# Two changes of order around the output blocks: a root of one number ahead of the statistics, and norm products inside the last matrix product

## What is computed

```
h = modulate(rms_norm_2(x, g_pre_mix[l]), sh1, sc1)
...
o = merge_branches(y_ml, y_ga, y_na, zg, w_branch[l], w_out[l])
x = x + ga1 * rms_norm_2(o, g_post_mix[l])
f = conv_ffn(modulate(rms_norm_2(x, g_pre_ffn[l]), sh2, sc2), w_up[l], conv_w[l], conv_b[l], w_down[l])
x = x + ga2 * rms_norm_2(f, g_post_ffn[l])
```

## Time and profile before

| what | value |
|---|---|
| runs | 1713.98, 1712.07, 1714.08 us, median 1713.98 |
| profiled execution, span | 1713.0 us |
| profiled execution, own time | not listed apart from its span |
| PE busy | 1674.3 us of the span (98%) |
| DVE busy | 1254.8 us (73%) |
| ACT busy | 841.9 us (49%) |
| ACT_TABLE_LOAD at L1456 | 4, of 1283 ns each |
| chain that ended last | PE 76%, DVE 15%, ACT 5%, issue 3% |

### The profile page before, as it was taken

The page is one execution under the profiler, slowest core; times in us unless marked ns, Lnnn a source line. Parts: engine busy times, 40 slices in busy tenths (PEclk is TensorE's granted clock), DMA queues, the critical chain, the costliest instruction groups (busy, mean ns, idle before and its releaser), DMA issues.

```text
span 1713.0 us, 25200 instructions
## 1 busy us (share of the span) xinstructions
PE 1674.3 (98%) x9808; PEld 1429.3 (83%) x9808; DVE 1254.8 (73%) x2194; ACT 841.9 (49%) x1362; POOL 0.2 (0%) x4
## 2 busy tenths in 40 slices
PE   9989989999999999999999999999999999999998
PEld 9888878777788778888888888888778989979987
DVE  7999767774779698856877776347756786678874
ACT  6665545563324344346444442336453455466653
POOL 0000000000000000000000000000000000000000
PEclk9999999999999999999999999999999999999999
DMA  8646542232224344542445556324322444547554
GB/s 340 225 160 237 191 138 87 77 145 62 63 94 171 110 147 168 207 151 99 139 133 196 197 196 221 98 75 136 99 86 62 130 151 147 174 154 171 196 187 133
DMA packets 79078, 254.91 MB, mean 149 GB/s; under 512 B 14320, under 2 KB 18672, under 8 KB 78320
## 3 DMA queue, kind: packets, MB, share of 16 engines
q1 hardware_dynamic: 73488, 244.91, 43.1%
q10 hardware_dynamic: 5472, 8.39, 1.5%
HBM read 252.19 MB, written 1.07 MB: 148 GB/s over the span
## 4 chain that ended last, share of the span: by engine, by line
PE 76%; DVE 15%; ACT 5%; issue 3%; DMA 0%; ACTq 0%; DVEq 0%
PE bank L713 63%; DVE w_lo L1792 4%; PE bank L856 2%; PE bank L1027 2%; PE bank L1013 2%; PE bank L1105 2%; PE bank L1004 2%; DVE mod_w L1848 1%; ACT w_hi L1215 1%; DVE probT L1848 1%; PE bank L1094 1%; DVE att L2382 1%; DVE xc L1891 1%; PE bank L750 0%; DVE resid_x L2248 0%
## 5 line engine op out<-in xcount | busy, mean ns | idle before, releaser
L1792 DVE TENSOR_TENSOR w_lo<-w_raw,w_hi 128x1024 fp32r<-128x1024 f32 (+1 forms) x356 | 426.8, 1211 | 254.7 <-ACT w_hi L1215 253.0
L1215 ACT ACTIVATE w_hi<-w_raw 128x1024 fp32r<-128x1024 f32 (+1 forms) x356 | 369.9, 1048 | 337.5 <-PE bank L713 284.2
L713 PE MATMUL bank<-hT_hi,w_hi 128*128 128x512 f32 (+1 forms) x1280 | 446.0, 348 | 1.7 <-issue 0.6
L713 PE MATMUL bank<-hT_hi,w_lo 128*128 128x512 f32 (+1 forms) x1280 | 437.5, 342 | 0.0
L713 PE MATMUL bank<-hT_lo,w_hi 128*128 128x512 f32 (+1 forms) x1280 | 437.3, 342 | 0.0
L713 PEld LDWEIGHTS bank<-hT_hi,w_hi 128*128 128x128 f32 x1280 | 242.7, 190 | 30.1 <-issue 3.1
L713 PEld LDWEIGHTS bank<-hT_hi,w_lo 128*128 128x128 f32 x1280 | 242.5, 189 | 28.2
L713 PEld LDWEIGHTS bank<-hT_lo,w_hi 128*128 128x128 f32 x1280 | 242.8, 190 | 27.0 <-issue 1.0
L1848 DVE SCALAR_TENSOR_TENSOR mod_w<-mod_w,c_rows 128x1024 f32<-128x1024 f32 x96 | 117.0, 1219 | 8.5 <-DMA mod_w<-in_mod_weights 8.5
L713 PE MATMUL bank<-w_hi,hT_hi 128*128 128x512 f32 x272 | 114.7, 422 | 0.0
L713 PE MATMUL bank<-w_lo,hT_hi 128*128 128x512 f32 x272 | 106.6, 392 | 0.0
(11 more groups left out here) (387 smaller groups left out, 2798.0 us busy)
## 6 DMA issues: line engine op xcount, KB each, us to landing
w_raw<-in_weights SPq DMA_DIRECT2D x356, 512.0 KB, 4.0
mod_w<-in_mod_weights SPq DMA_DIRECT2D x96, 512.0 KB, 4.1
nbias<-in_window_bias ACTq DMA_DIRECT2D x32, 128.0 KB, 2.9
resid_c<-in_ctx ACTq DMA_DIRECT2D x2, 1024.0 KB, 5.3
gain_mix<-gain_rows SPq DMA_DIRECT2D x3, 512.0 KB, 5.5
gain_ffn<-gain_rows SPq DMA_DIRECT2D x3, 512.0 KB, 4.3
c_rows<-in_conditions SPq DMA_DIRECT2D x1, 1024.0 KB, 5.8
gatew<-in_gate_weights SPq DMA_DIRECT2D x1, 1024.0 KB, 11.3
```

What stands on the lines that cost most here:

```text
L713: mm = pe.matmul(held[key][:, oc], st, mv_, start=(opens and k == 0 and t == 0 and i == 0), stop=(closes and k == tiles - 1 and t == 2), s ...
L1215: a.activation(w_hi[:, p % RING, :, used], w_raw[:, p % RING, :].rearrange("p (k n) -> p k n", k=KP)[:, :, used], ACT.Copy).then_inc(hi_re ...
L1792: v.tensor_tensor(w_lo[:, p % RING, :, used], w_raw[:, p % RING, :].rearrange("p (k n) -> p k n", k=KP)[:, :, used], w_hi[:, p % RING, :, ...
```

## The change

Three edits. First, in `output`, ahead of the first second-half statistics of each passage (c = 1, g = 0), ACT takes the root of one column of `eps` into a spare column, `rs[:, 60:61]`. Second, in the last layer's `wo`, `norm_T` for tile 2 is called through `within` with `before=1`: ahead of the last of tile 3's four pieces. Third, in the same passage (`early`), ACT and DVE do p = 0 and 1 of tile 2's norm ahead of their wait for tile 3's bank, and p = 2 between tile 3's statistics and its residual.

```diff
-                        if within and len(of) == 1 and of[0][0] == banks[-1][0] and p == n - 3:
+                        if within and len(of) == 1 and of[0][0] == banks[-1][0] and p == n - 1 - before:
...
-                             within=None if last or c == 0 else lambda: norm_T(0, "ffn", 0),
+                             within=None if c == 0 else lambda l=l: norm_T(l, "ffn", 0), before=1 if last else 2,
...
-                if last:
-                    norm_T(l, "ffn", 0)
...
+                        early = final and last and which == "mix"
                         if final:
                             split_hi(after + 2)
                             if two:
                                 norm_hi(*nxt, 0, 1)
+                            if early:
+                                split_hi(after + 3)
+                                for p in range(2):
+                                    norm_hi(*nxt, 0, p)
                         else:
                             ahead(key)
+                        if c == 1 and g == 0:
+                            a.activation(rs[:, 60:61], eps[:], ACT.Sqrt).then_inc(*A.next())
                         act.wait_ge(*filled_at(key))
...
-                            if final and not two:
+                            if final and not two and not early:
                                 norm_hi(*nxt, 0, 0)
...
-                            if final:
+                            if early:
+                                norm_hi(*nxt, 0, 2)
+                            elif final:
                                 split_hi(after + 3)
...
+                    early = final and last and which == "mix"
+                    if early:
+                        norm_tmp(*nxt, 0, 0)
                     if final:
                         split_lo(after + 2)
                         if two:
                             norm_lo(*nxt, 0, 1)
                             norm_tmp(*nxt, 0, 2)
+                        elif not early:
+                            norm_tmp(*nxt, 0, 0)
                         else:
-                            norm_tmp(*nxt, 0, 0)
+                            norm_lo(*nxt, 0, 0)
+                            norm_tmp(*nxt, 0, 1)
+                            norm_lo(*nxt, 0, 1)
...
+                    elif early:
+                        split_lo(after + 3)
+                        norm_tmp(*nxt, 0, 2)
...
+                    elif early:
+                        norm_lo(*nxt, 0, 2)
```

More of the change, by code:

```diff
@@ L679, in gemm @@
             def gemm(banks, tiles, x_hi, x_lo, weights_stationary, beside=None, inputs=None,
-                     by_bank=False, first_k=0, opens=True, closes=True, pool=None, within=None):
+                     by_bank=False, first_k=0, opens=True, closes=True, pool=None, within=None, before=2):
                 pool = pool or ("gemm" if beside else "rot")
@@ L1426, in output @@
             def output(l, which, w, tts, nxt):
+                last = l == LAYERS - 1
                 for c in range(2):
@@ L1475, in output @@
                                 split_hi(after + 4)
-                                if not two:
+                                if not two and not early:
                                     norm_hi(*nxt, 0, 2)
```

## The result

| kernel | median, us | lowest to highest | runs |
|---|---|---|---|
| before | 1712.45 | 1712.07 to 1714.65 | 20 |
| changed | 1715.36 | 1714.66 to 1717.61 | 20 |

The ratio is 1.0017, with a 95% interval of 1.0011 to 1.0023: 2.9 us slower (1.9 to 3.9). That is within the 0.2%, 3.4 us, that the prediction called no difference, though the interval reaches past it. It forecast +2.2 us.

The account below looks back on a forecast made before the run. PE, busy 98% of the span, bounds the kernel, so edits gain only its idling. First layer −0.88, last layer's mix passage +1.45, half clock +1.65 sum to +2.2 us on 1713.98: 1716.2 us, range 1712.8 to 1718.2.

Parts of the forecast that it names:

- half clock over the products: Last layer's mix passage: PE's stop brings 1.2 GHz during tile 3's products, +1.65 us; 1716.2 us in all, chance 0.53.
- The small root: Four output passages: table load hides in ACT's wait; first layer's mix passage gains 0.88 us, FFN and kernel's end nothing.
- Steps 1 and 2: Last layer's mix passage: tile 2's diagonal 0.88 us earlier; PE idles 1.09 us ahead of the first products.
- Steps 3 and 4: Last layer's mix passage: tile 3's bank ends 3.0 us later; DVE's sum of the halves comes 1.47 us later.
- the reason that I gave the greatest weight: Tile 3's bank can't be full before the products standing ahead of it, so it ends 3.0 us later.
- the rival that the cover works: Tile 3's statistics aren't held up; PE gains 0.88 us in each mix passage: 1712.2 us, chance 0.09.
- Steps 5 and 6: p = 0 and 1 run without idling; sum to diagonal takes 6.0 us; products 1.7 us later, PE idles 4.4 us.
- Step 6: Tile 3's chain from sum to diagonal: 6.0 us instead of 5.76, with `w_lo` 1.15 and p = 2's `ptmp` 0.65.
- The clock: The 4.4 us stop halves PE's clock; second products last about 3.45 us instead of 1.81, +1.65; bounds 0 and +4.
- The case that the half clock holds through p = 2 and 3: Last layer's mix passage: half clock lasts beyond the products, +2.4 us more; +4.6 in all, 1718.6 us, chance 0.13.
- The rival that the clock stays: Clock stays at 1.00 through the stop, as at 94: +0.57 us, 1714.5 us, chance 0.22.
- The level: Forecast difference of +2.2 us added to the runs' median of 1713.98 us: 1716.2 us.

Follow-up runs that it names:

- the order alone: Changed kernel with tile 2's norm products back behind the last piece of tile 3's bank, small roots and new ACT and DVE order kept: 1716.1 us, ratio 1.0021.
- the filled kernel: Changed kernel plus 18 matmuls of 128x128, results overwritten, between p = 1 and the wait for tile 3's diagonal: 1713.59 us, ratio 1.0003.

## Why the prediction was right

The forecast, half clock over the products, came true, at +2.9 instead of +2.2 us. Its steps:

- **The small root.** As forecast: the load hidden, DVE's inversion directly behind the gain product, 0.97 us in the first layer's mix passage for 0.88, one of PE's two waits gone and the other kept. In the first layer's FFN passage nothing was gained: 3.50 us early at its third Square (1142.58 after, 1146.08 in the earlier trace rows), 3.55 at the next passage (the 0.36 us from 3.14 to 3.50 are before's own, as said above). The root follows the load 0.01 us after its end (762.75 + 1.28, 764.04), and the passages gained 0.97 and 0.89 us, less than the 1.28 that the load itself takes. The Trainium skill (ScalarE: Activation LUTs, What ACT_TABLE_LOAD costs) adds 1380 ns of drain to each load; no run here shows any.
- **Steps 1 and 2.** PE's stop ahead of the first products was 0.93 us for 1.09. Right: from the slot behind the last matmul's start, as I had counted it, it is 1.09 (1505.96 + 0.23 to 1507.28).
- **Steps 3 and 4.** The sum of the halves came 1.79 us late where I said 1.47. The size was near, since I let ACT pass through p = 1 first. The bank was 3.0 us late, as forecast, but the reason that I gave the greatest weight was not the one that came last. With the bank early (the order alone) the diagonal is as late. With the bank late and the old order it is 2.0 us late instead of 3.0. I used the same reason against the rival that the cover works. That rival fails even where the bank is in time.
- **Steps 5 and 6.** p = 0 and 1 without idle time. From the sum to tile 3's products 6.13 us for 6.05. The stop was 4.70 for 4.4. Step 6 had what matters most for a repair, the `w_lo` and the `ptmp` moved onto the path; without them the kernel is 2.3 us faster. I priced them and did not ask which of the edit's parts was dispensable.
- **The clock.** It fell, and the products lost 1.62 us for the 1.65 forecast. It came back only within p = 2, which I had between the sum and its upper bound: against the filled kernel 0.5 us more. All of it is 2.1 us, 0.4 more than forecast. The later diagonal, 2.1 us for 1.7, is the rest of what the forecast was short of. The case that the half clock holds through p = 2 and 3 did not come about. The rival that the clock stays leaned on 94 in the earlier trace rows; of all eleven traces that one alone stayed at 1.00 there.
- **The level.** I added the difference to the 1713.98 of three runs; twenty put that median at 1712.45. So 1716.2 lies 0.8 above the measured 1715.36 although the difference was forecast 0.7 too small. I also took the profiled execution to lie 1.0 us below the median of the three, since its own time was not listed. It was some 2 us above the median of the twenty. That the level came out so near is luck in part: two errors of opposite sign.

## What to carry to other kernels

When a chain on two engines sets a passage, don't ask which consumer could start earlier. Ask what stands ahead of the item that is needed last. Here PE got p = 0 and 1 of tile 2 without a gap and then waited 4.7 us for tile 3's diagonal. Moving 0.65 us of work from ahead of that diagonal to behind it gained, where the whole rearrangement lost. Ask it of each input of that item: here the bank and the work ahead of it were each late enough alone, and with one of them mended two thirds of the delay, or all of it, were left. And gathering short stops of PE into one long one has a price of its own, for the long one may end at half the clock. Here the four stops of before, 3.1 us in all, ended at 1.00, and the one of 4.70 us cost 2.1 us by the clock alone.

## What the runs showed of the hardware

- A stop and the clock don't go together by length alone. In the passage of the last layer the granted clock stayed at 1.00 through stops of 1.32, 0.76 and 0.45 us and of 1.48 us in the kernel before. It fell within or behind stops of 4.70, 4.72, 4.17 and 3.07 us, behind one of 2.11 and once behind one of 1.81. Elsewhere one and the same stop ended both ways. That of 2.67 us ahead of 238.92 in before (237.12 in the changed kernel) ended at 0.50 before and at 1.00 after. That of 3.61 us ahead of 93.70 in before (93.06) ended at 1.00 before and at 0.50 after, and in the nine other traces the clock was at 0.50 to 0.79 in 94 to 96 too. Windows of before, then of the changed kernel:

```profile
240.00:242.00 2.00, 2.00 (x12) 2.00 (x11) 1.96 (x5) 0.65 (x2) 0.00 (x0) 0.50 0.00 0
```

```profile
92.00:94.00 2.00, 0.94 (x4) 0.97 (x5) 2.00 (x4) 1.98 (x3) 0.00 (x0) 0.74 0.17 55
94.00:96.00 2.00, 2.00 (x12) 2.00 (x11) 1.97 (x2) 1.99 (x3) 0.00 (x0) 0.50 0.56 219
238.00:240.00 2.00, 1.06 (x10) 0.82 (x8) 2.00 (x5) 0.90 (x2) 0.00 (x0) 1.00 0.00 0
```

- Such differences in the first 250 us shift the rest of an execution by some 2 us, which is as much as the edits here are worth. A single pair of profiled executions would have shown no change at all.
